# A decoder block with 64 experts: slots kept by token tile, each half gathered from its own tile, and the shared expert's down product in the first expert pass

## The reference

```python
scores = jax.nn.sigmoid(t @ w_router)                      # 256 tokens x 64 experts
...                                                        
_, eidx = lax.top_k(jnp.where(emask, biased, -jnp.inf), TOP_K)   # 8 experts per token
combine = ...                                              # weight of each token in each expert
gu = jnp.einsum('cd,edf->cef', tc, w_experts_gate_up)      # 1024 -> 2 x 256 for each expert
act = silu(gu[..., :256]) * gu[..., 256:] * cc[..., None]
routed = jnp.einsum('cef,efd->cd', act, w_experts_down)    # 256 -> 1024
shared = (silu(sgu[:, :256]) * sgu[:, 256:]) @ w_shared_down
return routed + shared
```

## Time and profile before

| | us |
|---|---|
| median of 3 runs | 731.45 |
| the profiled execution, device time | 729.72 |
| its span in the trace | 727.9 |
| PE busy | 665.2 |
| DVE busy | 303.9 |
| ACT busy | 165.3 |

### The profile page before, as it was taken

How to read it: one execution, slowest core, us unless ns; L and a number is a source line. 1 busy time by engine, 2 the same in 40 slices (tenths; PEclk the granted TensorE clock), 3 DMA queues, 4 the chain that set the end, 5 groups by cost and what they waited for, 6 DMA issues and landing times.

```text
span 727.9 us, 10005 instructions
## 1 busy us (share of the span) xinstructions
PE 665.2 (91%) x3371; PEld 375.5 (52%) x3371; DVE 303.9 (42%) x690; ACT 165.3 (23%) x292; POOL 34.1 (5%) x61
## 2 busy tenths in 40 slices
PE   2899999999999999989999988989989998899895
PEld 0478866888785487653434433434333433343342
DVE  2338989988233386342222223122231222213314
ACT  2010133213220241122322312123221322222211
POOL 7001111000000001000000000000000000000001
PEclk9999999999999999999999999999999999999997
DMA  8999989633410007526899999999999999999961
GB/s 303 387 387 324 390 306 341 243 128 128 172 64 0 1 3 302 218 93 255 341 429 422 427 423 427 431 425 426 427 422 429 425 426 429 422 430 420 427 289 58
DMA packets 43132, 225.65 MB, mean 310 GB/s; under 512 B 3488, under 2 KB 3520, under 8 KB 29414
## 3 DMA queue, kind: packets, MB, share of 16 engines
q1 hardware_dynamic: 41528, 224.43, 76.5%
q10 hardware_dynamic: 1582, 0.94, 0.5%
HBM read 224.31 MB, written 1.05 MB: 310 GB/s over the span
## 4 chain that ended last, share of the span: by engine, by line
PE 56%; DMA 34%; SPq 3%; DVE 3%; issue 1%; ACT 1%; ACTq 0%; DVEq 0%
DMA raw<-n_w_experts_gate_up_dram 31%; PE bank L1149 16%; PE bank L1483 13%; PE bank L1432 4%; PE bank L1288 4%; PE bank L1320 4%; PE bank L1467 3%; DMA ring<-in_w_in_dram 3%; PE bank L1177 2%; SPq L319 2%; PE bank L1473 1%; SPq L323 1%; PE bank L1491 1%; PE bank L1100 1%; PE bank L1400 1%
## 5 line engine op out<-in xcount | busy, mean ns | idle before, releaser
L1149 PE MATMUL bank<-work,ring 128*128 128x256 f32 x512 | 116.1, 384 | 1.7 <-DMA ring<-in_w_in_dram 1.7
L1483 PE MATMUL bank<-raw,hT 128*32 128x512 f32 x832 | 96.9, 619 | 19.7 <-DMA raw<-n_w_experts_gate_up_dram 19.7
L1149 PEld LDWEIGHTS bank<-work,ring 128*128 128x128 f32 x512 | 97.3, 192 | 17.3 <-issue 2.9
L1467 PE MATMUL bank<-raw,hT 128*128 128x512 f32 x224 | 101.6, 607 | 2.8 <-ACT hT L629 2.8
L1048 DVE TENSOR_TENSOR sg<-sg,bank 128x256 f32<-128x256 f32 x27 | 11.4, 421 | 169.8 <-ACT sg L638 169.8
L1483 PEld LDWEIGHTS bank<-raw,hT 128*32 128x32 f32 x832 | 30.6, 114 | 84.7 <-issue 84.7
L1467 PEld LDWEIGHTS bank<-raw,hT 128*128 128x128 f32 x224 | 42.1, 193 | 62.1 <-issue 60.4
L1443 PE MATMUL bank<-y,ST 128*128 128x512 f32 x224 | 71.0, 440 | 2.3 <-DVE y L1057 2.3
L1473 PE MATMUL bank<-raw,aT 128*128 128x512 f32 x112 | 51.7, 604 | 8.7 <-ACT aT L643 8.7
L647 ACT ACTIVATE y<-bank,wcol 128x512 fp32r<-128x512 f32 x54 | 34.1, 683 | 108.5 <-PE bank L1473 54.3
L638 ACT ACTIVATE sg<-bank 128x256 f32<-128x256 f32 x27 | 17.1, 634 | 182.4 <-PE bank L1483 99.2
(11 more groups left out here) (279 smaller groups left out, 582.3 us busy)
## 6 DMA issues: line engine op xcount, KB each, us to landing
raw<-n_w_experts_gate_up_dram SPq DMA_DIRECT2D x53, 2048.0 KB, 16.7
raw<-in_w_experts_down_dram SPq DMA_DIRECT2D x53, 1024.0 KB, 18.5
ring<-in_w_ada_dram SPq DMA_DIRECT2D x12, 2048.0 KB, 18.5
ring<-in_w_in_dram SPq DMA_DIRECT2D x9, 2048.0 KB, 13.1
ring<-in_w_out_dram SPq DMA_DIRECT2D x2, 2048.0 KB, 8.5
ring<-in_w_attn_out_dram SPq DMA_DIRECT2D x1, 2048.0 KB, 19.0
ring<-in_w_conv_out_dram SPq DMA_DIRECT2D x1, 2048.0 KB, 7.7
ring<-in_w_shared_gate_up_dram SPq DMA_DIRECT2D x1, 2048.0 KB, 7.9
```

What stands on the lines that cost most here:

```text
L1149: ins = mm(b[:, kk * SEQ:(kk + 1) * SEQ], w[:, k, m * PART:(m + 1) * PART], h1T[:, k, :], start=(k == 0), stop=(k == KD - 1))
L1467: ins = mm(psU[:, :], hT[:, k, :], wg[:, k, :], start=(k == 0), stop=(k == KD - 1))
L1483: ins = mm(psU[c:c + 32, :], hT[:, k, c:c + 32], w_gu(s)[:, k, :], start=(k == 0), stop=(k == KD - 1))
```

## The change

The slots now lie in two ranges: 0 to 1023 for the tokens of tile 0, sorted by expert, and 1024 to 2047 for tile 1. A block b of 512 slots needs only tile b // 2, so each k has two matmuls in place of four, and there is one `SS` for a block in place of two. An expert's slots are then two pieces, one in each range. `input_of` copies both: the low window first, then the high one behind it at an offset (`split_at`), over what the low copy wrote too much, so it waits for the low copies (`hT_low`). Each window thus takes three table entries (low, high, split) on ACT and two copies. ACT's copy to `aT` (`turned`) moves ahead of the input of the next pass. The shared down weights get a place of their own (`wshd`), so that the first SMALL load no longer waits for `shared_down`, and `shared_down` moves into the first pass in place of its `scatter`. PE's first round of the loop is written out ahead of it.

```diff
-    T_START, T_EXP = 2, 2 + CAND
+    T_EXP, T_OFF, T_LOW, T_HIGH, T_SPLIT = (2 + CAND * i for i in range(5))
...
-        hT = sb("hT", [PART, KD, PART])
+        hT = sb("hT", [PART, KD, 2 * PART])
...
+        wshd = sb("wshd", [PART, KF * D])
+        shT = sb("shT", [PART, KF, SEQ])[:, :, :]
...
-        def window_of(engine, j):
-            return engine.value_load(tab[0:1, bass.ds(j + T_START, 1)], min_val=0, max_val=SLOTS)
+        def offset_of(engine, j):
+            return engine.value_load(tab[0:1, bass.ds(j + T_OFF, 1)], min_val=0, max_val=PART)
+
+        def windows_of(engine, j, n):
+            low = engine.value_load(tab[0:1, bass.ds(j + T_LOW, 1)], min_val=0, max_val=TILE)
+            high = engine.value_load(tab[0:1, bass.ds(j + T_HIGH, 1)], min_val=TILE, max_val=SLOTS)
+            return low, high, engine.value_load(tab[0:1, bass.ds(j + T_SPLIT, 1)], min_val=0, max_val=n)
...
                 if s == SMALL[0]:
                     sp.wait_ge(*users[SHGU])
-                    sp.wait_ge(*users[SHD])
...
-            def big_input(g):
-                p = window_of(a, g)
-                a.activation(hT[:, :, :], hs[:, :, bass.ds(p, PART)], ACT.Copy).then_inc(hT_ready, 1)
-
-            def trio_input(g):
-                for s, c, n in TRIO_WINDOWS:
-                    p = window_of(a, trio_rank(s, g, n_big, n_trio))
-                    ins = a.activation(hT[:, :, c:c + n], hs[:, :, bass.ds(p, n)], ACT.Copy)
+            def input_of(windows, i):
+                wins = [(at, n) + windows_of(a, j, n) for j, at, n in windows]
+                for at, n, low, high, split_at in wins:
+                    ins = a.activation(hT[:, :, at:at + n], hs[:, :, bass.ds(low, n)], ACT.Copy)
+                ins.then_inc(hT_low, 1)
+                a.wait_ge(hT_low, i + 1)
+                for at, n, low, high, split_at in wins:
+                    ins = a.activation(hT[:, :, bass.ds(split_at + at, n)], hs[:, :, bass.ds(high, n)], ACT.Copy)
                 ins.then_inc(hT_ready, 1)
...
-            def outputs(i, down, count):
+            def turned(i):
                 a.wait_ge(t_done, i + 1)
                 a.activation(aT[:, :, :], psM[:, 0:F].rearrange("p (k n) -> p k n", k=KF), ACT.Copy).then_inc(aT_ready, 1)
+
+            def outputs(i, down, count):
...
                 a.wait_ge(big_gu, g + 1)
                 gate()
-                trio_input(g)
+                turned(g * 2)
+                trio_input(g, g * 2 + 1)
                 outputs(g * 2, big_dn, g + 1)
...
                     for s in range(2):
-                        for t in range(TH):
-                            ins = mm(bank[i % 2][:, :], h2r[s][:, t, k * PART:(k + 1) * PART], SS[:, q % 2, t, :],
-                                     start=(s == t == 0), stop=(s == 1 and t == TH - 1))
+                        ins = mm(bank[i % 2][:, :], h2r[s][:, b // 2, k * PART:(k + 1) * PART], SS[:, b % 2, :],
+                                 start=(s == 0), stop=(s == 1))
...
             def both(i):
-                pe.wait_ge(y_lo, i * 2 + 2)
-                scatter(PASSES[:5])
+                first_pass = isinstance(i, int) and i == 0
+                if first_pass:
+                    shared_down()
+                else:
+                    pe.wait_ge(y_lo, i * 2 + 2)
+                    scatter(PASSES[:5])
                 pe.wait_ge(act_ready, i + 1)
...
-            with pe.Fori(0, n_trio) as g:
+            pe.wait_ge(tabs_ready, 1)
+            big(0, 0)
+            trio(1, 0)
+            with pe.Fori(1, n_trio) as g:
```

More of the change, by code:

```diff
@@ L167, in hybrid_conformer_fox_moe_block @@
         gout = work[:, 4352:4368].rearrange("p (t g) -> p t g", t=TH)
[L168 to L173, removed]
+        ecnt = work[:, 4930:4932]
+        firsts = st2[:, 10:12]
+        ends = st2[0:E, 12:14]
         slotT = ST[0:E, :]
@@ L178, in hybrid_conformer_fox_moe_block @@
         perm = work[:, 5584:5712]
-        left, keycol, rank, startv = (work[:, 5712 + i:5713 + i] for i in range(4))
+        left, keycol, rank, high, split_at, skipped = (work[:, 5712 + i:5713 + i] for i in range(6))
         tcol = work[:, 5720:5723]
@@ L413, in _ @@
                                     pattern=[[-1, PART]], channel_multiplier=1))
+            link(pool.affine_select(out=before[:, :], in_=before[:, :], compare_op=ALU.not_equal, fill=SELECTED, base=0,
+                                    pattern=[[-1, PART]], channel_multiplier=1))
             link(pool.iota(pcol[:, :], pattern=[[0, 1]], base=0, channel_multiplier=1,
@@ L975, in _ @@
             v.wait_ge(ecum_done, 1)
[L976 to L994, removed]
+            link(v.scalar_tensor_tensor(firsts, ecnt, -SELECTED, bank[3][:, 448:450], ALU.mult, ALU.add))
@@ new lines, in _, with slots_turned @@
+            v.scalar_tensor_tensor(high, firsts[:, 1:2], float(TILE), skipped, ALU.add, ALU.subtract).then_inc(starts_in, 1)
+            v.wait_ge(experts_ps, 1)
+            v.tensor_copy(tab[0:1, T_EXP:T_EXP + 2 * CAND], bank[7][0:1, 0:2 * CAND]).then_inc(experts_ready, 1)
+            def slots_turned(t):
+                v.tensor_scalar(slotT[:, t * PART:(t + 1) * PART], bank[3][0:E, t * PART:(t + 1) * PART],
+                                firsts[0:E, t:t + 1], -SELECTED, ALU.add, ALU.add).then_inc(slotT_ready, 1)
@@ L995, in emat @@
+            slots_turned(0)
+            link(v.tensor_tensor(ends, firsts[0:E, :], ecnt[0:E, :], ALU.add))
+            def emat(b):
+                t, at = divmod(b, 2)
+                bs, js = slice(b * W, (b + 1) * W), slice(at * W, (at + 1) * W)
+                link(v.tensor_scalar(Emat[:, bs], iota[0:E, js], ends[:, t:t + 1], None, ALU.is_ge))
+                v.scalar_tensor_tensor(Emat[:, bs], iota[0:E, js], firsts[0:E, t:t + 1], Emat[:, bs].bitcast(fp32),
                                        ALU.is_ge, ALU.subtract).then_inc(E_ready, 1)
-            v.wait_ge(slotT_ps, 1)
@@ L1016, in _ @@
             v.wait_ge(tally_ready, 1)
[L1017 to L1022 removed]
+            for b in range(4):
+                for i in range(KD * b + 1, KD * (b + 1), 2):
+                    if i == KD * b + 3 and b < 3:
+                        emat(b + 1)
+                    if i == KD * b + 5 and b < 3:
+                        select(b + 1)
                     v.wait_ge(gather_ps, i + 1)
[L1024 removed]
+                    v.tensor_copy(hs[:, i % KD, b * W:(b + 1) * W], bank[1][:, :]).then_inc(gather_out_dve, 1)
             n_trio, n_big = loop_counts(v)
@@ L1366, in _ @@
                     mm(bank[0][c:c + E, 448:449], sel[:, t, :], ones[:, 0:1], start=(t == 0), stop=(t == TH - 1))
+                for t in range(TH):
+                    mm(bank[0][c:c + E, 449 + t:450 + t], sel[:, t, :], ones[:, 0:1], start=True, stop=True)
             for t in range(TH):
@@ L1453, in both @@
                 ins.then_inc(t_done, 1)
-                scatter(PASSES[5:])
+                if not first_pass:
+                    scatter(PASSES[5:])
                 pe.wait_ge(si_ready, i + 1)
```

154 lines of the change are left out of this document (82 added, 72 removed).

## The result

The changed kernel takes 768.95 us (median of 4 runs, 767.76 to 769.91), the kernel before in the same comparison 732.21 us (4 runs, 729.86 to 733.39). The ratio is 1.0505, 95% interval 1.0483 to 1.0528: slower by 36.7 us. The forecast was 769, slower.

What follows compares the result with a forecast made beforehand. Prediction: the weights' stream sets the rounds' pace before; after, ACT's loads ahead of `hT` do. Span 727.9 - 2.3 up to the first trio product + 25.6 rounds + 16.9 clock = 768.1, plus 1.8: 769 us; 8-in-10 range 746 to 780.

Steps and rivals of the forecast that it cites:

- Ahead of the gather: Stretch before the gather: added small products, less two turnings, cost +1.0 us, bounds 0 and +1.4.
- The gather: Gather: 64 of 128 matmuls go, `shared_down` leaves, `Emat` comes late; together -15.0 us, bounds -21.9 and -6.9.
- The banks' round: Gather: one bank's round of matmuls and copy out falls from 1.97 to 1.52 us, the copy remaining.
- Into the first pass: From the gather's last copy to the first pass: two more table entries and a second copy on ACT, +2.4 us.
- The first pass: From PE's first product to the first trio product: 25.3 us instead of 15.95, +9.3 us.
- ACT's path: Big pass, `t_done` to trio product: nine loads behind `aT`, then six copies, 9.3 us, bounds 8.7 and 9.8.
- The rounds: Twelve expert rounds: 31.3 us each, above the 29.5 the weights ask, so the stream no longer binds; +25.6 us.
- The trio pass: Same ACT path in a trio pass, three loads and two copies, 4.7 us from `t_done`: +0.2 us.
- The clock: Trio products behind `hT` waits: 10 of 13 run at lower clock, 1.7 us each, +16.9 us, bounds 0 and 22.
- Had the loads run ahead: Rival, chance 0.08: ACT's sequencer works off its loads while `aT` waits; rounds stay with the stream, 721 us, faster.
- Had the clock held: Rival, chance 0.06: ACT's path as forecast but PE's clock holds; 752 us, or down to 744 with loads at 0.6.
- The gather at PE's rate: Rival in the gather: it goes at PE's own rate, 7 us less, 762 us; no chance of its own given.

Runs made afterwards that it cites:

- the filled wait: Changed kernel with eight unread 128x256 products into an unused half bank ahead of PE's wait for `hT` in each trio pass: 743.35 us, ratio 1.0155.
- the seven experiments that contain the change: All follow-up runs built on the changed kernel, from 714.58 to 840.55 us; only the kernel before with nine loads is not among them.
- the two traces of kernels without it: The kernel before, and the kernel before with `aT` copied first and each table entry loaded three times with single copies, 741.28 us, ratio 1.0125.
- Four banks: Changed kernel with the gather going round four PSUM banks in place of two: 764.58 us, ratio 1.0451.
- the last experiment: Changed kernel with all table loads early, also the first input's, four gather banks, and `Emat` made one copy earlier: 714.58 us, ratio 0.976.
- `shared_down` moved: Changed kernel with `shared_down` in the first pass behind the turning of the activations instead of ahead of it: 763.86 us, ratio 1.0439.
- the loads early: Changed kernel with ACT's table loads for the next input moved ahead of its wait for the pass's first product: 724.68 us, ratio 0.9903.

## Why the prediction was right

Every number here is from the profiled executions, by the prediction's own terms; they are compared on the span (727.9 to 767.9, +40.0).

**Ahead of the gather: +4.1, where +1.0 was said and +1.4 was the bound.** The gather starts at 285.02 instead of 280.93. Part is the program: from the 40 matmuls ahead of the routing's small products to the gather PE needed 15.6 us before (265.29 to 280.93) and 18.2 after (266.81 to 285.02). Of these 2.6 us, 1.1 are the added products, as the trace of the filled wait shows, where the stretch takes 16.7 (266.79 to 283.49). The other 1.5 are a lower granted clock while PE was busy for all of the stretch; the windows after and with the filled wait:

```profile
275.00:280.00 5.00, 5.00 (x30) 4.17 (x28) 1.79 (x10) 0.16 (x1) 1.91 (x8) 0.66 0.00 0
```

```profile
275.00:280.00 5.00, 5.00 (x41) 4.00 (x41) 3.25 (x13) 0.16 (x1) 2.23 (x8) 1.00 0.00 0
```

The stretch up to the gather takes 18.2 in six of the seven experiments that contain the change, and 15.6 in the two traces of kernels without it; the prediction left this clock out. The last 1.5 us lie ahead of those 40 matmuls, whose start differs between executions by as much: 265.15 to 266.81 in the eight traces with the change, 265.29 and 268.74 in the two without.

**The gather: -15.3 for -15.0.** 26.35 us for 41.6 (280.93 to 322.55). The banks' round is 1.52 us, as worked out: 64 of 128 matmuls are gone and the copy stays. Four banks show the rest of the argument.

**Into the first pass: +2.0 for +2.4.** From the end of DVE's last copy to PE's product it is 4.08 us (311.37 to 315.45), before 2.06.

**The first pass: +8.9 for +9.3.** It takes 24.9 us (315.45 to 340.34). Up to the first trio product all this sums to -0.3, where -2.3 was said; the trace has it at 340.34 for 340.56, which is -0.2.

**ACT's path: 8.5 us for 9.3.** This is the step on which the forecast rested, and its mechanism holds, though the length lies below the bound of 8.7. The gate's load did not run ahead, and the nine loads don't either: the first starts 0.11 after `aT`. Taken apart in the second big pass (the rows above): 0.05 to `aT`; 5.75 to the first copy, where 5.94 was said; 3 low copies in 1.25, not 1.5, since they overlap; 0.15 to the high ones, 1.26 for these; and PE follows 0.06 after them, not 0.34. In the first big pass it is 8.7. PE's wait is 4.1, not 4.7. The Trainium skill, Perfetto Trace Analysis, section Sequencer Loop, has the sequencer go on past an instruction that waits in the engine's queue. On that the forecast differed from the page, and the trace agrees with the forecast: ACT's registers were loaded only once `aT` had begun.

**The rounds: +14.2 for +25.6.** At full clock a round takes 30.4 us, as the filled wait measures it, not 31.3; twelve of them are 364.6 - 350.4 = +14.2. Of the 0.9 us a round that were too many, 0.8 are ACT's path. The trio pass, from which 0.2 was expected, adds nothing: PE has no wait ahead of the big products in the rounds.

**The clock: +26 for +16.9, where 22 was the bound.** All 13 waits were followed by the lower clock, where 10 were assumed, and at 2.0 us each, where 1.7 were: the products take 8.5 and 9.7 in turn where 7.07 is the full clock. Filling the waits gave 25.6 us back in device time. The Trainium skill, TensorE: Matmul & The Clock Gate, section on how HAM oscillation bites in real kernels, has the lower clock behind every such wait. The trace of the change agrees, 13 of 13 at 4.1 to 4.6 us. Waits of 2.2 us, on which that section says nothing, were followed by it in 8 of 13 and 10 of 13 cases here.

The sum of what was measured is -0.3 + 14.2 + 26 = +39.9; the trace has +40.0. Against the forecast's +40.2 the measured terms are off by +2, -11 and +9. The mechanism and the sign held. The sizes of the rounds and of the clock did not, each was off by a third or more, and the clock came out the larger of the two. That the total lies within 0.2 us is luck.

**The rivals.** Had the loads run ahead, 721 us were said; with the loads moved ahead by hand the kernel takes 724.7, so the rival's price was right within 4 us and its premise wrong. Had the clock held, 744 to 752 were said; with the wait filled it is 743.4. The gather at PE's rate was said to save 7 us; four banks, which allow that rate, save 4.4, as `Emat` comes late. With `Emat` made earlier too, in the last experiment, the gather is 7.9 us shorter.

**What stays open.** Why the clock is lower at 275 to 280 us in seven of the eight traces with the change and not in the one with the filled wait, though PE waits for nothing there, was not tried. Just ahead of it (271.6 to 274.6) stand the routing's small products, to which the change adds a few; that they are the cause is not shown. Nor is it shown what decides which of the waits of equal length is followed by the lower clock: behind waits of 3.1 to 3.3 us for weights it was 4 of 7 in the last experiment.

## What to carry to other kernels

Where ACT reads addresses from a table at run time, count the loads behind each waiting instruction: in every round here they began only when its wait was over. Moving such loads ahead of the waits took 44 us off the kernel and left no wait for `hT` in the rounds. When an engine has slack against a stream of weights, say how much, and price the clock with it: a wait that would still fit into the slack at full clock can be followed by the lower clock and then doesn't. And when work is taken out of a loop that hands banks on, work out the round with the copy in it, since the copy and whatever stands between two copies become the bound.

## What the runs showed of the hardware

- In the rounds ACT took 0.61 to 0.71 us from one table load to the next with its address arithmetic, in one place 0.92, with nothing computed beside them; ahead of the first pass it took 0.53.
- A load behind an instruction that waits did not start during the wait: it came 0.10 us after the start of a gate that had waited 5.69 us, and 0.10 to 0.11 us after the start of `aT` in each of the 13 rounds of the change.
- Waits of 4.1 to 4.6 us ahead of a product were followed by the lower clock in 13 of 13 cases (12 of 12 with `shared_down` moved). Waits of 2.2 to 2.5 us were in 10 of 13 and 8 of 13. Waits of 3.0 to 3.3 us for weights were in 5 of 5 cases with the loads early, and in 4 of 7 with four banks as well.
- Behind repeated waits of 4.1 us the loss was 1.5 and 2.6 us in turn. Behind waits of 2.2 us it was 1.7 or nothing.
- Eight products of 128x256 nobody reads, 3.6 us of work in a wait of 4.1 us, kept PE at full clock and made the kernel 25.6 us faster than without them.
